# A two-layer decoder trunk: small row-spread products and the split of the scaled memory are put in other places of a hand-written order

## What is computed

```python
h = rmsnorm(x, g_mix[l])
z = h @ w_in[l]
c_b, c_c, c_v, q, k, v, f_logit = jnp.split(z, SPLITS, axis=-1)
y_conv = short_gated_conv(c_b, c_c, c_v, conv_w[l])
y_conv = rmsnorm(y_conv.reshape(B, S, CONV_GROUPS, HEAD_DIM), ...)
q = rmsnorm(q.reshape(B, S, FOX_HEADS, HEAD_DIM), g_q[l])
k = rmsnorm(k.reshape(B, S, FOX_HEADS, HEAD_DIM), g_k[l])
log_f = jax.nn.log_sigmoid(f_logit + b_f[l])
y_fox = forgetting_attention(q, k, v, log_f)      # 8 heads x 64, causal
y_fox = rmsnorm(y_fox, ...)
x = x + jnp.concatenate([y_conv, y_fox], axis=-1) @ w_out[l]
hx = rmsnorm(x, g_xa[l])
m = rmsnorm(mem, g_mem[l])
x = x + mem_cross_attention(hx, m, w_xq[l], w_xkv[l], ...) @ w_xo[l]   # 4 heads x 128
```

## Time and profile before

| | |
|---|---|
| median of 3 runs | 1502.49 us (1500.33, 1502.49, 1509.77) |
| the profiled execution | 1510.66 us, span 1509.1 us |
| mean granted TensorE clock | 0.953 |
| TensorE busy | 1412.8 us (94%) |
| VectorE busy | 987.3 us (65%) |
| ScalarE busy | 809.9 us (54%) |
| GpSimd busy | 89.2 us (6%) |

### The profile page before, as it was taken

One profiled execution on the slowest core, in us unless ns is written; L12 is line 12 of the kernel. 1 busy time (PEld: TensorE's weight loads), 2 busy tenths in 40 slices (PEclk: granted clock), 3 DMA queues, 4 the chain that ended last, 5 costly groups with the idle time before them and its releaser, 6 DMA issues.

```text
span 1509.1 us, 19337 instructions
## 1 busy us (share of the span) xinstructions
PE 1412.8 (94%) x7577; PEld 1208.6 (80%) x7577; DVE 987.3 (65%) x749; ACT 809.9 (54%) x704; POOL 89.2 (6%) x92
## 2 busy tenths in 40 slices
PE   5998987999988998978699999999999999999998
PEld 5997665999978987575588888888888888888786
DVE  5436335445455364333488888888888978889788
ACT  4424125334344434132467876777767777677674
POOL 2020000000000020001000000000000000000300
PEclk9999788999998987887799999999999999999999
DMA  9413143464468321222699999999999999999994
GB/s 304 140 64 112 56 139 139 155 209 154 154 240 318 126 84 56 84 104 77 232 371 344 402 389 348 379 351 398 389 348 382 348 401 383 348 389 343 401 389 186
DMA packets 126485, 386.28 MB, mean 256 GB/s; under 512 B 7796, under 2 KB 61664, under 8 KB 126432
## 3 DMA queue, kind: packets, MB, share of 16 engines
q1 hardware_dynamic: 114544, 365.08, 64.7%
q0 software_dynamic: 3168, 11.54, 2.0%
q10 hardware_dynamic: 8720, 8.91, 1.7%
HBM read 369.78 MB, written 15.73 MB: 255 GB/s over the span
## 4 chain that ended last, share of the span: by engine, by line
PE 73%; DVE 10%; DMA 5%; ACT 5%; issue 4%; POOL 1%; SPq 1%; DVEq 0%; ACTq 0%; POOLq 0%
PE bank L1407 42%; PE bank L1403 14%; PE bank L1404 14%; DVE wl L1011 4%; DMA ring<-in_we_down 2%; ACT wh L726 2%; DVE wl L992 2%; DMA ring<-in_we_gate 2%; PE bank L1782 1%; ACT aT L742 1%; DVE xl L1017 1%; DMA ring<-in_we_up 1%; DMA rows_of<-xn,rows 1%; DVE scratch L1124 1%; DVE scratch L1107 0%
## 5 line engine op out<-in xcount | busy, mean ns | idle before, releaser
L1011 DVE TENSOR_TENSOR wl<-ring,wh 128x2816 fp32r<-128x2816 f32 (+1 forms) x127 | 400.4, 3173 | 62.5 <-PE bank L1407 39.3
L726 ACT ACTIVATE wh<-ring 128x2816 fp32r<-128x2816 f32 (+1 forms) x128 | 337.1, 2633 | 126.1 <-DMA ring<-in_we_down 44.4
L992 DVE TENSOR_TENSOR wl<-ring,wh 128x3072 fp32r<-128x3072 f32 (+2 forms) x53 | 164.2, 3101 | 156.6 <-ACT wh L712 147.4
L1403 PE MATMUL bank<-wh,xh 128*128 128x512 f32 x528 | 200.7, 380 | 21.0 <-ACT wh L726 13.9
L1011 DVE TENSOR_TENSOR wl<-ring,wh_third 128x2816 fp32r<-128x2816 f32 (+1 forms) x64 | 187.1, 2923 | 32.5 <-PE bank L1407 27.5
L1404 PE MATMUL bank<-wh,xl 128*128 128x512 f32 x528 | 199.2, 377 | 0.0
L1407 PE MATMUL bank<-wl,xh 128*128 128x512 f32 (+1 forms) x768 | 195.4, 376 | 0.0
L712 ACT ACTIVATE wh<-ring 128x3072 fp32r<-128x3072 f32 (+1 forms) x52 | 128.3, 2470 | 108.7 <-PE bank L1407 51.9
L726 ACT ACTIVATE wh_third<-ring 128x2816 fp32r<-128x2816 f32 (+1 forms) x64 | 155.8, 2434 | 43.9 <-DMA ring<-in_we_up 21.5
L1407 PEld LDWEIGHTS bank<-wl,xh 128*128 128x128 f32 x768 | 142.3, 188 | 18.5
L1403 PEld LDWEIGHTS bank<-wh,xh 128*128 128x128 f32 x528 | 99.9, 189 | 43.3 <-issue 17.7
(11 more groups left out here) (261 smaller groups left out, 2070.8 us busy)
## 6 DMA issues: line engine op xcount, KB each, us to landing
ring<-in_we_gate SPq DMA_DIRECT2D x64, 1408.0 KB, 7.7
ring<-in_we_up SPq DMA_DIRECT2D x64, 1408.0 KB, 8.1
ring<-in_we_down SPq DMA_DIRECT2D x56, 1536.0 KB, 8.9
ring<-in_w_in SPq DMA_DIRECT2D x16, 1536.0 KB, 8.5
ring<-in_w_gate SPq DMA_DIRECT2D x6, 1536.0 KB, 7.4
ring<-in_w_up SPq DMA_DIRECT2D x6, 1536.0 KB, 6.6
ring<-in_w_down SPq DMA_DIRECT2D x6, 1536.0 KB, 6.4
rows_of<-zeros ACTq DMA_DIRECT2D x1, 8704.0 KB, 41.4
```

Of the source, the lines that this page charges most:

```text
L726: nc.scalar.activation(wh_in_pass(j, n), ring[:, slot, 0:n], ACT.Copy).then_inc(high_ready, 1)
L992: nc.vector.tensor_tensor(wl[:, j, 0:n], ring[:, slot, 0:n], wh[:, j, 0:n].bitcast(F32), ALU.subtract).then_inc(low_ready, 1)
L1011: nc.vector.tensor_tensor(wl[:, j % 2, 0:n], ring[:, j % NSLOT, 0:n], wh_in_pass(j, n).bitcast(F32), ALU.subtract).then_inc(low_ready, 1)
L1403: nc.tensor.matmul(dst, x_high, w_high, start=first, stop=False)
```

## The change

It moves work within the streams and splits one step over three engines:
- `bq`: the spreads of q and k run after `conv2`, ahead of `conv3`, and VectorE's four gains go ahead of its subtract for `z` 7. The forget biases of heads 4 to 7 go between the two halves of the scores.
- The means `ssc` and `ssmk` run between the first and the second half of the memory values; ScalarE's evictions of the values go behind the guesses.
- `bc` and `bmk`: these spreads run behind the products with v, ahead of the projection; VectorE's readers of them move accordingly.
- The scaled memory has a place of its own in `scratch`, and GpSimd multiplies it once the forget result `f` is full. After `conv5` ScalarE rounds it in two pieces (768 and 1280 columns), GpSimd subtracts the first piece and VectorE the second; `memg_ready` counts two.
- Layer 1 starts with a load of the ScalarE table that holds both logarithm and exponential.

```diff
@@ -69,10 +69,10 @@
     if layer == 0:
         names += [f"mT{i}" for i in range(4)]
     names += [f"qk{i}" for i in range(4)] + ["v0", "v1", "ssqk"]
-    names += [f"conv{i}" for i in range(6)] + [f"bq{i}" for i in range(4)]
+    names += [f"conv{i}" for i in range(3)] + [f"bq{i}" for i in range(4)] + [f"conv{i}" for i in range(3, 6)]
     names += [f"s{h}" for h in range(8)]
-    names += ["mk0", "mk1", "mv0", "mv1", "ssc", "ssmk"] + [f"pt{h}" for h in range(4)]
-    names += ["bc0", "bc1", "bmk0", "bmk1"] + [f"pt{h}" for h in range(4, 8)] + ["o0", "o1"]
+    names += ["mk0", "mk1", "mv0", "mv1", "ssc", "ssmk"] + [f"pt{h}" for h in range(8)]
+    names += ["o0", "o1", "bc0", "bc1", "bmk0", "bmk1"]
     names += [f"wo{i}" for i in range(4)] + ["oT0", "oT1"]
     names += [f"yT{i}" for i in range(4)] + ["xq0", "xq1"]
     names += ["xs0", "xs1", "xqm", "xs2", "xs3"] + [f"xpt{h}" for h in range(4)] + ["xo0", "xo1"]
@@ -249,7 +249,7 @@
         pT = part(9216, FH, 3 * P)
         otok = part(12288, TT, FH * HD)
         ksq = part(12288, XH, S)
-        mem_gained = xn[:].rearrange("p t (k s) -> p (t k) s", s=S)
+        mem_gained = part(10240, KT, S)
         yT = xn[:].rearrange("p t (k s) -> p (t k) s", s=S)
         xsc = part(5120, XH, 2, S)
         xpT = part(9216, XH, 2, S)
@@ -626,14 +628,16 @@
                     pool.wait_ge(meansq_ready, norms)
                     rstd(msq[:, 2:4])
 
-                pool.wait_ge(*full(l, "conv5"))
+                pool.wait_ge(*full(l, "f"))
                 if l == 0:
                     pool.wait_ge(*taken(0, "vec"))
                     for i in range(4):
                         pool.wait_ge(*taken(0, f"mT{i}"))
-                then_wait(nc.gpsimd.tensor_tensor(mem_gained, memT[:], bcast_last(col(l, "mem", 0, KT), S), ALU.mult))
-                then_wait(nc.gpsimd.tensor_copy(aT[:], mem_gained))
-                nc.gpsimd.tensor_tensor(aT_low[:], mem_gained, aT[:].bitcast(F32), ALU.subtract).then_inc(memg_ready, 1)
+                nc.gpsimd.tensor_tensor(mem_gained, memT[:], bcast_last(col(l, "mem", 0, KT), S), ALU.mult).then_inc(mem_scaled, 1)
+                pool.wait_ge(mem_scaled, l + 1)
+                pool.wait_ge(mem_high, 2 * l + 1)
+                nc.gpsimd.tensor_tensor(aT_low[:, 0:3, :], mem_gained[:, 0:3, :], aT[:, 0:3, :].bitcast(F32), ALU.subtract
+                                        ).then_inc(memg_ready, 1)
                 pool.wait_ge(osum_ready, l + 1)
                 rstd(mfox[:])
                 norms += TT
...
@@ -756,6 +760,7 @@
                     nc.scalar.dma_start(rows_of.rearrange("(p a) (b c) -> p (a b) c", p=P, c=256),
                                         zeros[:].unsqueeze(1).to_broadcast([P, (2 * NE + 1) * (D // 256), 256])
                                         ).then_inc(rows_cleared, 16)
+                    nc.scalar.preload_act_table_set("natural_log_exp_and_others")
                     high_of(l, "z", 0)
                 mean_squares(l, ["d0", "d1", "d2", "d3"])
                 if l == 1:
@@ -798,7 +803,12 @@
                                          ACT.Copy).then_inc(take(l, f"conv{i}"), 1)
                     if i in (0, 2):
                         high_of(l, "z", 6 + i // 2)
-                high_of(l, "xkv", 0, 1)
+                high_of(l, "xkv", 0)
+                act.wait_ge(mem_scaled, l + 1)
+                act.wait_ge(*full(l, "conv5"))
+                for a, b in ((0, 3), (3, KT)):
+                    nc.scalar.activation(aT[:, a:b, :], mem_gained[:, a:b, :], ACT.Copy).then_inc(mem_high, 1)
+                high_of(l, "xkv", 1)
 
                 for h in range(FH):
                     act.wait_ge(negmax_ready, 4 * l + 2 * (h // 4 + 1))
@@ -815,13 +825,13 @@
                 for i in range(2):
                     act.wait_ge(*taken(l, f"mk{i}"))
                 square(l, "mk", ksq, xk[:])
-                for i in range(2):
-                    act.wait_ge(*full(l, f"mv{i}"))
-                    nc.scalar.activation(xv[:, i, :], bank(l, f"mv{i}")[:], ACT.Copy).then_inc(take(l, f"mv{i}"), 1)
                 act.wait_ge(conv_ready, l + 1)
                 square(l, "cv", zc[:, 4:8, :], zc[:, 0:4, :])
                 guess_rows(l, "cv", "ssc", mcv[:])
                 guess_rows(l, "mk", "ssmk", mmk[:])
+                for i in range(2):
+                    act.wait_ge(*full(l, f"mv{i}"))
+                    nc.scalar.activation(xv[:, i, :], bank(l, f"mv{i}")[:], ACT.Copy).then_inc(take(l, f"mv{i}"), 1)
                 for h in range(1, FH, 2):
                     act.wait_ge(*full(l, f"pt{h}"))
                     nc.scalar.activation(pT[:, h, :], bank(l, f"pt{h}")[:, 0:3 * P], ACT.Copy).then_inc(take(l, f"pt{h}"), 1)
@@ -1090,18 +1100,22 @@
                         ins.then_inc(decay_ready, 1)
                 low_of(l, "z", 4, 5)
                 refine_rows(l, "qk", "ssqk", mqk[:])
-                low_of(l, "z", 6, 7)
-                for i in range(2):
-                    dve.wait_ge(*full(l, f"conv{4 + i}"))
-                    dve.wait_ge(*taken(l, f"conv{2 + i}"))
-                    u = zc[:, 4 + 2 * i:6 + 2 * i, :].rearrange("p a s -> p (a s)")
-                    nc.vector.tensor_tensor(u, bank(l, f"conv{4 + i}")[:], u, ALU.mult).then_inc(take(l, f"conv{4 + i}"), 1)
+                low_of(l, "z", 6)
                 for i in range(4):
                     dve.wait_ge(*full(l, f"bq{i}"))
                     qk = zqk[:, 2 * i:2 * i + 2, :].rearrange("p a s -> p (a s)")
                     nc.vector.scalar_tensor_tensor(qk, qk, col(l, "q" if i < 2 else "k"), bank(l, f"bq{i}")[:],
                                                    ALU.mult, ALU.mult).then_inc(take(l, f"bq{i}"), 1)
-                low_of(l, "xkv", 0)
+                low_of(l, "z", 7)
+                for i in range(2):
+                    dve.wait_ge(*full(l, f"conv{4 + i}"))
+                    dve.wait_ge(*taken(l, f"conv{2 + i}"))
+                    u = zc[:, 4 + 2 * i:6 + 2 * i, :].rearrange("p a s -> p (a s)")
+                    nc.vector.tensor_tensor(u, bank(l, f"conv{4 + i}")[:], u, ALU.mult).then_inc(take(l, f"conv{4 + i}"), 1)
+                    if i == 0:
+                        low_of(l, "xkv", 0)
+                dve.wait_ge(mem_high, 2 * l + 2)
+                act_low(aT_low[:, 3:KT, :], mem_gained[:, 3:KT, :], aT[:, 3:KT, :]).then_inc(memg_ready, 1)
                 for h in range(FH):
                     dve.wait_ge(*full(l, f"s{h}"))
                     nc.vector.scalar_tensor_tensor(sc[:, h, :], bank(l, f"s{h}")[:, 0:3 * P], HD ** -0.5, mask[:],
...
@@ -1540,15 +1550,16 @@
                     for c in (2 * i, 2 * i + 1):
                         channel_tile(ps[:, (c % 2) * S:(c % 2) * S + S], (l, "z", 4 + c // 3), ZCOLS, (c % 3) * P, c % 3 == 2,
                                      done(l, f"conv{i}") if c % 2 else None)
+                    if i == 2:
+                        pe.wait_ge(rows_ready, ROWS[l, "qk"])
+                        spread_rows(l, "bq", spreadg[:], mqk[:], 8)
                 pe.wait_ge(decay_ready, l + 1)
                 forget_bias(l, range(4))
-                pe.wait_ge(rows_ready, ROWS[l, "qk"])
-                spread_rows(l, "bq", spreadg[:], mqk[:], 8)
-
                 for i in range(4):
                     pe.wait_ge(*taken(l, f"bq{i}"))
-                forget_bias(l, range(4, FH))
                 for j in range(FH // 2):
+                    if j == 2:
+                        forget_bias(l, range(4, FH))
                     for h in (2 * j, 2 * j + 1):
                         r = (h % 2) * HD
                         mm(bank(l, f"s{h}")[:, 0:P], zqk[r:r + HD, j, 0:P], zqk[r:r + HD, 4 + j, 0:P], False, False)
@@ -1557,7 +1568,7 @@
                         mm(bank(l, f"s{h}")[:, P:3 * P], zqk[r:r + HD, j, P:S], zqk[r:r + HD, 4 + j, :], False, True
                            ).then_inc(done(l, f"s{h}"), 1)
 
-                pe.wait_ge(memg_ready, l + 1)
+                pe.wait_ge(memg_ready, 2 * l + 2)
                 for i in range(2):
                     ps = open_bank(l, f"mk{i}")
                     for c in range(2):
@@ -1567,9 +1578,10 @@
                         ps = open_bank(l, f"mv{t}") if s == 0 else bank(l, f"mv{t}")
                         token_tile(ps[:, 256 * s:256 * s + 256], (l, "xkv", 2 + s), 256, 0, 256, t, t == TT - 1,
                                    done(l, f"mv{t}") if s else None)
-                pe.wait_ge(squares_ready, SQUARES[l, "cv"])
-                mean_rows(l, "ssc", selg, 14, 8, zc[:, 4:8, :], 4)
-                mean_rows(l, "ssmk", selh, 3, 4, ksq, XH)
+                    if s == 0:
+                        pe.wait_ge(squares_ready, SQUARES[l, "cv"])
+                        mean_rows(l, "ssc", selg, 14, 8, zc[:, 4:8, :], 4)
+                        mean_rows(l, "ssmk", selh, 3, 4, ksq, XH)
                 def probs_transposed(heads):
                     for h in heads:
```

(11 more changed lines are left out.)

41 lines of the change are left out of this document (20 added, 21 removed).

## The result

The changed kernel took 1488.04 us (median of 5 runs, 1485.36 to 1490.73); the kernel before, in runs beside it, 1509.15 (5 runs, 1500.33 to 1512.14). The ratio on record is 0.989, interval 0.986 to 0.992; these two medians alone give 0.986. Counted over all runs of this study the kernel before has a median of 1504.12 us (65 runs, 1496.3 to 1513.6, one run at 2018 left out) and the changed kernel 1489.09 us (11 runs, 1483.9 to 1492.5). The change gains **15.0 us**. Forecast were 25.6 and 1477 us.

What follows compares the result with a forecast made beforehand. TensorE was taken as the bound, busy 94% of the span, losing time to idleness and half clock. Gains of 11.0 us in layer 0 and 14.6 in layer 1, together 25.6, gave 1477 us against the 1502.49 median; range 1465 to 1492.

Steps and rivals of the forecast that it cites:

- S3: mcv and mmk spreads behind the products with v: 29.3 us against 33.7 and 37.3, gaining 4.4 and 8.0 us by layer.
- S1: q and k spreads into the convolution products, memory split over three engines: 9.9 us against 14.1, gaining 4.2 us per layer.
- S2: Means between the memory values: 30.2 us against 32.7 and 32.5, gaining 2.4 us per layer.
- the third rival: VectorE and GpSimd hinder each other by the full 3.25 us, delaying masks, taps, means: 1483, up to 1490; chance 0.10.
- The first: Rival: products with v pull the clock down themselves, 4.6 us lost per layer, 1486 us; chance 0.15.
- The second: Rival: no clock dips at all by spreads or the gap, 6.0 us more gained per layer, 1465 us; chance 0.10.
- the sign that the prediction named for it: VectorE's 1280-column subtract taking above 2 us, listed among the signs that the forecast is wrong.
- The fourth: Rival: spreads amid convolution products keep the clock down for the six tiles behind, 31 us in both layers, 1508; chance 0.05.
- The fifth: Rival: TensorE's gain is lost waiting at the projection's weights or the next norm, about 1495 us; chance 0.05.

Runs made afterwards that it cites:

- S1 with the memory split: Kernel before with q and k spreads amid the convolution products and the scaled memory split over three engines, nothing else moved: 1504.99 us, ratio 0.999.
- before again: The kernel before, unchanged, run for a second trace: 1504.43 us, ratio 1.001.
- S1 without the split: Kernel before with q and k spreads ahead of conv3 and VectorE's gains moved along, scaled memory as before: 1511.45 us, ratio 1.005.
- S2 and S3 together: Kernel before with means between the memory values and the other spreads behind the products with v; q and k spreads and scaled memory unmoved: 1487.01 us, ratio 0.988.
- full-height spreads: Spreads made over all 128 rows, added rows zero: in the changed kernel 1474.67 us, in the kernel before 1488.39 us.

## Why the prediction was wrong by 11 us

**The step that failed** is the last of the sum: "it stood 8.2 us above the median of 1502.49, and against the median it is 1477". The gain was worked out in one execution and taken whole from a median of others. The profiled execution stood 6.5 us above the median of 65 runs, and in it a stretch of 16.9 us at half clock lay over the products with v in layer 0. In the other trace of before it is 3.3 us long, and the attention part of layer 0 is 6.6 us shorter (132.2 for 138.8). S3 ends just this stretch, so its 4.4 us in layer 0 contained the excess that was then subtracted as if it had nothing to do with the change. Had it been counted once, the forecast would have been 1510.66 - 25.6 = 1485.1, whatever the median.

How sure is that? The other execution with such a stretch in layer 0, that of S1 with the memory split, stood 5.3 us above its median; those of before again and of S1 without the split, where it is shorter, stood 2.1 above and 2.7 below theirs. That fits, but it is four executions, and others of the kernel before weren't traced: runs differ in more than this stretch.

The rest of the difference is that the profiled execution of after was a fast one, 3.7 us below its kernel's median: 25.3 - 6.5 - 3.7 = 15.1. The trace without the preload shows what such 3.7 us can consist of: attention parts longer by 3.1 and 1.8 us, by other dips, and 1.1 us less outside them.

Read by medians alone, the miss looks different: S2 and S3 together are worth 17.1 us (forecast 17.2), and S1 is worth -2.1, nothing that can be read, where 8.4 were forecast. In the traces the 17.1 isn't the forecast's (S2 and S3 took 11.7 and 14.3 us off the trace of before, 5.2 and 14.3 off the other), so that agreement is luck. But that S1's term was mis-sized holds by either reading; it doesn't show in the total of the traces only because the idle time that S1 causes had been charged to S2.

**Point by point**, forecast and the trace after (layers 0 and 1):
- *S1*, 9.9 us: spreads and dip 3.8 and 6.8 (by the same two marks as above), and 5.0 and 5.0 to the first memory product, so 8.8 and 11.9. The dip, priced at a loss of 1.7, is none in layer 0 and 6.7 us at half clock in layer 1, a loss of 3.4. VectorE's and GpSimd's subtracts came nearly as worked out:

```profile
107.45 2.00 ACT L810 ACTIVATE aT<-scratch 128x768 fp32r<-128x768 f32 x2 [7.68 <-PE bank L1417]
...
108.44 1.84 POOL L639 TENSOR_TENSOR aT_low<-scratch,aT 128x768 fp32r<-128x768 f32 x1 [67.63 <-ACT aT L810]
...
109.49 2.14 DVE L1026 TENSOR_TENSOR aT_low<-scratch,aT 128x1280 fp32r<-128x1280 f32 x1 [1.41 <-ACT aT L810]
```

  VectorE's 1280 columns end 4.4 us after the first bias (forecast 4.1). But the price stood on its own rows only. What it is worth in this kernel is the difference of two kernels, and that is nothing (1487.0 without it). What had been left out: most of the idle time before the means, which the forecast named under S2, is there only because S1 brings TensorE to the means sooner than VectorE can finish the taps (2.31 us with S1, 0.44 and 1.29 without).
- *S2*, 30.2 us: 30.9 and 29.2. The idle time was 2.31 for a forecast 2.6, with 3.3 us at half clock behind it in layer 0 and none in layer 1.
- *S3*, 29.3 us: 28.8 and 28.8. Products with v 5.47 (5.4), the last dip 6.7 and 6.8 us long, which is the loss of 3.4 us that it was priced at. The price that was wrong is that of the other side, 33.7 and 37.3: one draw of something that varies.
- The parts don't add: S1 1505.0, S3 1507.3, both near or above before, S2 with S3 1487.0. The sum was made as if each were worth the same alone.
- The range's upper end of 1492 isn't what a gain of 17 us gives (1485); only the third rival's 1490 comes near it.

**The rivals.** The first (products with v pull the clock down) is false: they ran at full clock in every trace that had means between the values. The second (no dips, 1465; the Trainium skill, "TensorE: Matmul & The Clock Gate", Part 1, has the clock follow how busy the engine is) is wrong about the dips: they are there with TensorE busy 6.70 of 6.70 us, so the rule as that page words it doesn't describe this kernel. Its time was also too low. With full-height spreads, which leave one dip in layer 0, the order gives 1474.7; the 1468.3 has the key means in front too. The third, that VectorE comes late, didn't happen in its form, though the sign that the prediction named for it did: the 1280 columns took 2.14 us, above 2, and ended 0.3 us late, not 3.25. The fourth (six slow convolution tiles) was seen in part, a loss of 3.4 of the 17.3 us in layer 1, and in the trace without the preload in both layers. The fifth didn't happen: outside the attention parts the traces of before and after agree within 0.6 us (1228.2 and 1228.8; over all traces 1227 to 1232).

**Where the gain is from.** With the clock kept up in both, the orders differ by 13.7 us (1488.4 and 1474.7), with the dips by 15.0. Full height gives 15.6 us in the old order and 14.4 in the new one. So the gain doesn't hang on the clock: of the 13.7 us, 12.4 are idle time of TensorE in the traces (18.3 us in the two attention parts, and 5.9). It doesn't follow that the dips are as many as before. In the two attention parts together the clock is down for 68 us in the first trace of before, 51 in the second and 27 after. But in the old order part of that lay over waits that come back when the clock is up: in the old order TensorE is idle for 13.9 and 15.5 us with the dips, and for 18.3 without. The forecast took some 5 us per layer from the clock in the products with v alone.

## What to carry to other kernels

Before a gain read in one profiled execution is subtracted from a median, ask what makes that execution longer than the median; if it lies in the stretch that is to be shortened, it counts once. Price a move by what the work lay under before it as well as by what it lies under after it, and price parts in the state that the other parts leave. Where small products feed the rest, try their shape before their place: 128 rows with zeros for 16, 8 and 4 gave as much in the old order as the whole reordering (1488.4 and 1489.1), and both together 1474.7.
